# Gate rows by way of device memory: a scratch row and a broadcast transfer in place of diagonals times ones on TensorE

## The reference

```python
def second_block(x, c, ...):
    c_act = jax.nn.silu(c)
    mod = (c_act @ w_mod[l] + b_mod[l])[:, None, :]
    sh_m, sc_m, g_m, sh_f, sc_f, g_f = jnp.split(mod, 6, axis=-1)
    h = rmsnorm_2(x, mix_pre_w[l]) * (1 + sc_m) + sh_m
    y = hybrid_mixer(h, w_in[l], ..., w_out[l])
    x = x + g_m * rmsnorm_2(y, mix_post_w[l])
    h = rmsnorm_2(x, ffn_pre_w[l]) * (1 + sc_f) + sh_f
    y = conv_ffn_2(h, w_up[l], ffn_conv_w[l], w_down[l])
    x = x + g_f * rmsnorm_2(y, ffn_post_w[l])
```

## Time and profile before

| | us |
|---|---|
| median of three runs | 2290.96 (2290.7 to 2292.55) |
| the profiled execution, its own time | 2292.63 |
| its span, first to last instruction | 2290.8 |
| PE busy | 2241.1 (98%) |
| DVE busy | 1615.6 (71%) |
| ACT busy | 1141.4 (50%) |

### The profile page before, as it was taken

One profiled execution on the slowest core, in us unless ns is written; L12 is line 12 of the kernel. 1 busy time (PEld: TensorE's weight loads), 2 busy tenths in 40 slices (PEclk: granted clock), 3 DMA queues, 4 the chain that ended last, 5 costly groups with the idle time before them and its releaser, 6 DMA issues.

```text
span 2290.8 us, 32511 instructions
## 1 busy us (share of the span) xinstructions
PE 2241.1 (98%) x12468; PEld 1954.0 (85%) x12468; DVE 1615.6 (71%) x1868; ACT 1141.4 (50%) x1363; POOL 76.1 (3%) x49
## 2 busy tenths in 40 slices
PE   7999999999999999999899999979999999999998
PEld 7879887888888888888898999768888888888886
DVE  5579677788888767767755666777888666665555
ACT  5454544555455554444536445545455554544444
POOL 0005200000000000000000110000000000000000
PEclk9999999999999999999999999999999999999999
DMA  8657375787878766878475454665887555555553
GB/s 294 222 178 258 129 257 210 248 286 282 283 275 287 257 193 231 299 277 308 163 252 182 152 166 147 240 219 191 287 286 271 177 185 192 191 184 201 185 200 110
DMA packets 190435, 512.92 MB, mean 224 GB/s; under 512 B 12201, under 2 KB 14201, under 8 KB 166409
## 3 DMA queue, kind: packets, MB, share of 16 engines
q1 hardware_dynamic: 190169, 511.51, 64.3%
q10 hardware_dynamic: 176, 0.14, 0.0%
HBM read 509.52 MB, written 2.10 MB: 223 GB/s over the span
## 4 chain that ended last, share of the span: by engine, by line
PE 95%; DVE 3%; ACT 1%; issue 0%; DMA 0%; POOL 0%; DVEq 0%; ACTq 0%
PE ps L1660 28%; PE ps L1618 16%; PE ps L1620 16%; PE ps L1619 16%; PE ps L1665 15%; DVE w_lo L963 1%; PE ps L1765 1%; PE ps L1932 1%; DVE region L1064 0%; ACT w_hi L498 0%; DVE region L1199 0%; PE ps L1987 0%; DMA region<-in_attn_norm_g 0%; ACT region L572 0%; DVE x L1523 0%
## 5 line engine op out<-in xcount | busy, mean ns | idle before, releaser
L963 DVE TENSOR_TENSOR w_lo<-raw,w_hi 128x1024 fp32r<-128x1024 f32 x768 | 954.3, 1251 | 609.0 <-ACT w_hi L498 608.2
L498 ACT ACTIVATE w_hi<-raw 128x1024 fp32r<-128x1024 f32 x768 | 810.0, 1059 | 923.8 <-PE ps L1620 509.0
L1660 PE MATMUL ps<-a_hl,w_hi 128*128 128x512 f32 x2816 | 706.4, 393 | 0.5 <-DVE a_hl L1054 0.5
L1660 PEld LDWEIGHTS ps<-a_hl,w_hi 128*128 128x128 f32 x2816 | 506.9, 189 | 92.2 <-issue 1.5
L1618 PE MATMUL ps<-w_hi,a_hl 128*128 128x512 f32 x1280 | 501.1, 391 | 2.2 <-DVE a_hl L1077 2.2
L1620 PE MATMUL ps<-w_hi,a_hl 128*128 128x512 f32 x1280 | 498.2, 389 | 0.0
L1619 PE MATMUL ps<-w_lo,a_hl 128*128 128x512 f32 x1280 | 498.1, 389 | 0.0
L1665 PEld LDWEIGHTS ps<-a_hl,w_lo 128*128 128x128 f32 x2816 | 384.2, 190 | 27.5
L1665 PE MATMUL ps<-a_hl,w_lo 128*128 128x256 f32 x2816 | 392.7, 282 | 0.0
L1618 PEld LDWEIGHTS ps<-w_hi,a_hl 128*128 128x128 f32 x1280 | 240.3, 188 | 54.4 <-issue 4.8
L1620 PEld LDWEIGHTS ps<-w_hi,a_hl 128*128 128x128 f32 x1280 | 240.3, 188 | 50.0
(11 more groups left out here) (187 smaller groups left out, 841.6 us busy)
## 6 DMA issues: line engine op xcount, KB each, us to landing
raw<-in_w_up SPq DMA_DIRECT2D x176, 1024.0 KB, 5.1
raw<-in_w_mod SPq DMA_DIRECT2D x96, 1024.0 KB, 5.0
raw<-in_w_in SPq DMA_DIRECT2D x88, 1024.0 KB, 5.1
raw<-in_w_down SPq DMA_DIRECT2D x88, 1024.0 KB, 4.9
raw<-in_w_out SPq DMA_DIRECT2D x32, 1024.0 KB, 5.2
x<-in_x SPq DMA_DIRECT2D x2, 1024.0 KB, 6.7
out_x<-x SPq DMA_DIRECT2D x4, 512.0 KB, 2.7
c_row<-in_c SPq DMA_DIRECT2D x1, 1024.0 KB, 9.7
```

Source lines behind the costliest of these rows:

```text
L498: nc.scalar.activation(w_hi[:, hh % HL_SLOTS, :], raw[:, n % RAW_SLOTS, half * HALF:(half + 1) * HALF], ACT.Copy).then_inc(hi_ready, 1)
L963: v.tensor_tensor(w_lo[:, hh % HL_SLOTS, :], raw[:, n % RAW_SLOTS, half * HALF:(half + 1) * HALF], w_hi[:, hh % HL_SLOTS, :].bitcast(F32), ...
L1660: mmul(dst[:, BLOCK * ft:BLOCK * (ft + 1)], w_hi[:, hh % HL_SLOTS, columns(kk, ft)], a_hl[:, kt, :, :].rearrange("p l s -> p (l s)"), star ...
```

## The change

The row no longer passes through PE, PSUM and ACT's copy. DVE makes the 16 columns of factors only (`gains`). ACT issues a DMA that writes them to a scratch row of 2048 floats in device memory (`row_out`; there are two such rows, `gate_rows`), and some chunks later a DMA that reads that row into all 128 partitions of `g_row` (`row_in`, which first waits on ACT until the write has landed). For the first row the steps stand in `in2`: `gains` after chunk 40, `row_out` after chunk 42, `row_in` after chunk 45. For the second they stand in `up2`: `gains` and `row_out` after chunk 41, `row_in` after chunk 44. `diag`, the matmuls, the copy and PE's four waits around them are gone.

```diff
-        diag = reg(20480, 2048).rearrange("p (k f) -> p k f", k=KT)
         g_row = reg(18432, 2048)
+        rows = nc.dram_tensor("gate_rows", (2, D), F32).ap()
...
+            def row_out(q):
+
+                act.wait_ge(sem("gains_ready"), q + 1)
+                with nc.allow_non_contiguous_dma(reason="a vector from columns to a row"):
+                    act.dma_start(rows[q].rearrange("(k p) -> p k", p=P), sm(GP, KT)).then_inc(sem("row_out"), 16)
+
+            def row_in(q):
+
+                act.wait_ge(sem("row_out"), 16 * (q + 1))
+                act.dma_start(g_row, rows[q].rearrange("(o d) -> o d", o=1).partition_broadcast(P)).then_inc(sem("row_ready"), 16)
...
+                if at == 42:
+                    row_out(0)
+                if at == 45:
+                    row_in(0)
...
-            def gate_row(q):
-
-                act.wait_ge(sem("row_mm"), q + 1)
-                nc.scalar.activation(g_row, ps[:, SIDE:SIDE + 2048], ACT.Copy).then_inc(sem("row_ready"), 1)
...
-                if at == 43:
-                    gate_row(1)
+                if at == 41:
+                    row_out(1)
+                if at == 44:
+                    row_in(1)
...
-            def gate_diag(wcols, first):
+            def gains(wcols, first):
 
                 dve.wait_ge(sem("modc_ready"), first // 4 + 4)
-                link(v.tensor_tensor(sm(GP, KT), modc[:, first:first + KT], wcols, ALU.mult))
-                v.tensor_tensor(diag, ident.unsqueeze(1).to_broadcast([P, KT, P]), sm(GP, KT).unsqueeze(2).to_broadcast([P, KT, P]),
-                                ALU.mult).then_inc(sem("diag_ready"), 1)
+                if first > 32:
+                    dve.wait_ge(sem("row_out"), 16)
+                v.tensor_tensor(sm(GP, KT), modc[:, first:first + KT], wcols, ALU.mult).then_inc(sem("gains_ready"), 1)
...
-            def gate_row(q):
-                pe.wait_ge(sem("diag_ready"), q + 1)
-                for n in range(4):
-                    mm = mmul(side(n), ones, diag[:, 4 * n:4 * n + 4, :].rearrange("p k f -> p (k f)"), start=True, stop=True)
-                mm.then_inc(sem("row_mm"), 1)
...
-            def first_row(at):
-                if at == 3:
-                    pe.wait_ge(sem("yT_gla_ready"), 8)
-                    gate_row(0)
-                if at == 7:
-                    pe.wait_ge(sem("row_ready"), 1)
...
-                if at == 42:
-                    pe.wait_ge(sem("up_summed"), 32)
-                    gate_row(1)
-                if at == 43:
-                    pe.wait_ge(sem("row_ready"), 2)
```

More of the change, by code:

```diff
@@ L910, in epi_sums @@
                                          accum_out=sm(P_SS + 4 * t + j)).then_inc(sem("post_sq"), 1)
-            def first_row(at):
-                if at == 5:
-                    gate_row(0)
-            pairs("out2", epi_sums, between=first_row)
+            pairs("out2", epi_sums)
             lead("up2", range(2))
@@ L1479, in mixer2 @@
                     mix_taps(0, 41 - at, at - 39)
+                if at == 40:
+                    gains(colA(A_MPOST, KT), 32)
                 if at == 43:
@@ L1501, in epi_gated @@
                 dve.wait_ge(sem("post_sq"), 2 * j + 2)
-                dve.wait_ge(sem("row_ready"), 1)
+                dve.wait_ge(sem("row_ready"), 16)
                 v.tensor_tensor(y[:, :, BLOCK * j:BLOCK * (j + 1)], main(blk).rearrange("p (t n) -> p t n", t=TT),
@@ L1505, in epi_gated @@
                                 ALU.mult).then_inc(epi_done, 1)
[L1507 to L1511, removed]
+            pairs("out2", epi_gated)
             lead("up2", range(2))
@@ L1530, in last_row @@
                 if at == 41:
-                    gate_diag(colB(B_FPOST, KT), 80)
+                    gains(colB(B_FPOST, KT), 80)
             up("up2", 1, last_row)
             down("down2", 1, "up2")
-            dve.wait_ge(sem("row_ready"), 2)
+            dve.wait_ge(sem("row_ready"), 32)
             for t in range(TT):
@@ L1982, in mixer2, with later_tiles2 @@
                     mm.then_inc(sem("o_turned"), 1)
-            def gate_row(q):
-                pe.wait_ge(sem("diag_ready"), q + 1)
-                for n in range(4):
-                    mm = mmul(side(n), ones, diag[:, 4 * n:4 * n + 4, :].rearrange("p k f -> p (k f)"), start=True, stop=True)
-                mm.then_inc(sem("row_mm"), 1)
-            pairs("in2", GATE_RANK, mixer2)
-            def first_row(at):
-                if at == 3:
-                    pe.wait_ge(sem("yT_gla_ready"), 8)
-                    gate_row(0)
-                if at == 7:
-                    pe.wait_ge(sem("row_ready"), 1)
-            pairs("out2", between=first_row)
+            pairs("in2", GATE_RANK, mixer2)
+            pairs("out2")
             norm(3, range(0, 4))
-            def last_row(at):
+            def later_tiles2(at):
                 if at == 0:
                     norm(3, range(4, 8))
-                if at == 42:
-                    pe.wait_ge(sem("up_summed"), 32)
-                    gate_row(1)
-                if at == 43:
-                    pe.wait_ge(sem("row_ready"), 2)
-            pairs("up2", between=last_row, summed=22)
+            pairs("up2", between=later_tiles2, summed=22)
             down("down2", 1, 2)
```

## The result

The changed kernel takes 2283.57 us in the median of its runs, against 2290.96 before; the ratio is 0.9968, with a 95% interval of 0.9959 to 0.9978. That is 7.39 us less; 2284.1 was forecast, in a range of 2282.5 to 2287.5. (One of the seven executions of the changed kernel took 4596.3 us; it stands in no comparison.)

What follows compares the result with a forecast made beforehand. PE, busy 98% of the span, was taken to bound the kernel between the norms. Removing the gate rows' matmuls takes away 6.88 us and the additions cost 0, so 2290.96 - 6.88 = 2284.1 us, range 2282.5 to 2287.5.

Steps and rivals of the forecast that it cites:

- TensorE's time: Gate-row matmuls in `out2` and `up2`: removing them gives 3.44 us of PE at each place, together 6.88 us.
- The removed work of DVE and ACT at 0: Diagonals (2 x 2.29 us) and ACT's copies (2 x 1.89 us) lay beside PE, so removing them was counted at 0.
- The 7.96 us stall of ACT: In `up2`, ACT stood 7.96 us before its gate-row copy without PE waiting; the stall was to be gone.
- The landing of the write: Scratch-row write in `in2` and `up2`: lands in 7.7 us, bounds 5.3 and 14.4, with no wait on ACT.
- under 15: Sign to look for in the profile: DMA landing of `gate_rows` under 15 us.
- The cover: Time from the write's issue until ACT reaches `row_in`: 18.2 us at the first place, 15.2 at the second.
- The 10.6 to 15.4 us: Landing if the write took twice L432's time; said to be still just in time at both places, sum unchanged.
- The other end of the issue, 5.03: Upper price of issuing `row_in` on ACT, from SP's broadcast of `c`: costs 1.4 us in `in2`, nothing in `up2`.
- The DMA engines: `row_in` moves 1 MB in about 7.5 us; a load beside it may take twice 5.1; cost 0, bounds 0 to 1.
- The late write: Rival: write lands after 21.4 us (first place) or 23.8 (second), PE runs dry; 2302.9 at 32 us; chance 0.04.
- Held ACT: Rival: broadcast issue holds ACT (2285.5), or write lands at 22 to 25 us (2285 to 2289); chance 0.12 together.
- the returned gain: Rival: loads set the pace of `out2`, so the first row's 3.44 us goes again, 2287.5; chance 0.05.

Runs made afterwards that it cites:

- extra: Changed kernel with both diagonals on DVE and a copy of the same size on ACT put back, the eight matmuls left out: 2283.84 us, ratio to before 0.9967.
- contig: Changed kernel with the first row's columns turned on TensorE, copied by ScalarE and written as 16 pieces of 512 B, `row_in` directly behind: 2284.02 us.
- sooner: Changed kernel with `row_in` one chunk earlier at both places: 2283.4 us.
- behind: Changed kernel with an added 1 MB broadcast of `c` issued directly behind the first `row_out`, without a wait between: 2284.28 us.
- land: Changed kernel with `row_in` directly behind `row_out`, at chunk 42 of `in2` and chunk 41 of `up2`: 2296.21 us, ratio to before 1.0022.
- tight: Changed kernel with `row_out` and `row_in` both at the late place, behind chunk 45 of `in2` and chunk 44 of `up2`: 2294.25 us, ratio 1.0014.
- no_rows: Changed kernel without making either gate row (no gains, writes or broadcasts; sums multiply by whatever lies in the buffer): 2284.11 us.
- first_only: Changed kernel with only the first row through device memory, the second made on TensorE as before: 2287.15 us, against 2290.94 before.

## Why the prediction was right, point by point

**TensorE's time.** Right: 6.88 forecast, 6.89 between marks, 6.87 against the profile with the same start, 3.8 and 3.3 alone. The medians moved by 7.39 and 7.28. The 0.4 above 6.88 is under what these runs can tell (the interval of the first is 5 to 9.4 us), and stays unexplained.

**The removed work of DVE and ACT at 0.** Right: put back, it costs 0.2. The 7.96 us stall of ACT is gone, and gave nothing.

**The landing of the write.** The mis-sized term. I chose 7.7 from L432, with 5.3 and 14.4 as bounds; it is 11.0 to 14.7, at its end above my bound of 14.4, and the sign "under 15" held by 0.3. What makes it longer at one place than at the other is not shown. The longest of these are in `up2`, where the kernel has 14.3 us: nothing to spare. In the profiled run of the changed kernel `row_in` goes out in time there (1781.43, as the rounding starts); in that of `extra` it is 0.2 us behind, after 14.5 us, and in that of `contig`, whose second row is the changed kernel's, 0.4 us behind, after 14.7. That costs nothing, since over 4 us of hold cost nothing in `sooner`. The cover itself was 0.9 us too long at both places, since ACT's queue issues a DMA while the engine is still at the instruction before.

The Trainium skill's rule, in "DMA: Bandwidth & Descriptors", rules for kernel authors, that a last dimension that isn't contiguous makes one descriptor per element, agrees with the 4096 added packets, and the contiguous write bears out its advice: 1.4 us against 11.1. The other line of that page of the Trainium skill, that pieces under 512 B are read, modified and written, is not shown by itself; the pieces of L432, 64 B, are short too, but go the other way. The 10.6 to 15.4 us that I made of it, by doubling, hold the measured 11.0 to 14.7, so it would have been the better choice of the two. But 15.4 would not have been "just in time at both places", as I wrote: I had given the second place 15.2. The 9.0 us for which ACT can be held there are what covers it, and what covered the 14.7.

**`row_in`.** Issue 0.34 to 0.35 (0.4 said), landing 7.4 and 7.8 (7.5 said). The other end of the issue, 5.03, did not come (0.93 in `behind`).

**The DMA engines.** The broadcast was the smaller matter; I had not counted that the pieces of `row_out` fill the engines. Windows of the changed kernel from its issue on:

```profile
1392.00:1398.00 6.00, 6.00 (x53) 6.00 (x52) 2.77 (x3) 2.32 (x3) 0.00 (x0) 1.00 0.26 4
1398.00:1404.00 6.00, 6.00 (x53) 6.00 (x52) 4.72 (x4) 3.96 (x7) 0.00 (x0) 1.00 0.77 44
1404.00:1410.00 6.00, 6.00 (x53) 6.00 (x52) 4.03 (x6) 3.85 (x5) 0.00 (x0) 1.00 0.95 338
```

A share of 0.77 for 44 GB/s: weight loads stand behind the pieces. The loads issued beside them landed in 13.5 and 11.3 us in `in2` (the first takes 5.0 in the kernel before, the second 5.1 in the kernel with 16 pieces) and in 11.7 and 11.1 in `up2`. I had said twice 5.1 for a load beside `row_in`, and the one issued 3.4 us ahead of it took 10.4. ACT has a wait of 2.1 us in all for loads of `out2` that it did not have. It cost 0, as said, since PE still had halves in hand.

**The rivals.** The late write (0.04) was less far off than I made it, since the kernel is at the edge of ScalarE being held; but time is lost only from a landing of 21.4 and 23.8 us, and the longest seen is 14.7. Its mechanism is real: `land` and `tight` are it, and they are slower than before. Its price was too low, for I counted only PE's wait; with the clock behind it, TensorE pays 1.5 to 2.5 us more for waits of 2.45 to 6.3 us. Held ACT (0.12) and the returned gain (0.05) are refuted by `no_rows` and `first_only`.

## What to carry to other kernels

Work that a bound engine does only to rearrange a few kilobytes can go through device memory, and its full time comes back if the read stands far enough behind the write (here three chunks of 5.6 us, for a landing of 11 to 15) and the use far enough behind the read; price the work by starts around it, between marks, and not by a difference of two spans. Where the pieces are short, count them: here 64 ns for each on each of 16 engines, and the weight loads stand behind them. And a wait of TensorE is priced with the clock behind it: here 0.3 us more than its length for 1.4 us, 1.5 to 2.5 more for 2.45 to 6.3.

## What the runs showed of the hardware that I had not expected

- ACT's queue issues a DMA while its engine is at an earlier instruction, ahead of an activation that stands before it in the program (`row_in` at 1409.33, L590 at 1410.28). A DMA that reads what the activation writes must wait for it by a semaphore, as the kernel with 16 pieces does.
- 2048 writes of 4 B land in 11.0 to 14.7 us and 16 of 512 B in 1.4. Four DMAs of 2048 pieces in a row block the issuing queue for 15.8 us, where one takes 0.41.
- An idle stretch of TensorE of 2.45 us was enough for the granted clock to fall to 0.56 to 0.59 over the next 4 us; behind one of 1.4 us it stayed at 1.00.
- Beside 2048 short pieces in ACT's queue, a weight load of 1 MB in SP's queue landed in 13.5 us instead of 5.0.
